# Dummy matmuls in TensorE's pauses, a reordered top-k schedule, and the first top-k quarter split by head, in a fused transformer and expert-lookup kernel

## The reference, cut to what matters

```python
def peer_ffn(h, wq, sub_keys, u, v):
    ...
        q = (xb @ wq).reshape(PEER_BLOCK, PEER_HEADS, 2, PEER_HALF)       # 128 tokens, 8 heads
        s = jnp.einsum('thpd,hpnd->thpn', q, sub_keys).astype(jnp.float32)
        s1, i1 = lax.top_k(s[:, :, 0], PEER_TOPK)                          # 16 of 128, twice
        s2, i2 = lax.top_k(s[:, :, 1], PEER_TOPK)
        cand = (s1[..., :, None] + s2[..., None, :]).reshape(PEER_BLOCK, PEER_HEADS, PEER_TOPK * PEER_TOPK)
        ...
        top, pos = lax.top_k(cand, PEER_TOPK)                              # 16 of 256
        eid = jnp.take_along_axis(cand_id, pos, axis=-1).reshape(PEER_BLOCK, PEER_HEADS * PEER_TOPK)
        g = jax.nn.softmax(top, axis=-1)...
        act = jax.nn.gelu(jnp.einsum('td,ted->te', xb, u[eid]))
        return jnp.einsum('te,ted->td', g * act, v[eid])
```

## Time and profile before

| what | value |
|---|---|
| median of 3 runs | 2390.88 us (2390.44 to 2392.16) |
| the profiled execution | 2392.13 us, of which the span is 2390.3 us |
| busy share: TensorE, VectorE, ScalarE, GpSimd | 85%, 63%, 32%, 42% |
| mean granted TensorE clock | 0.945 |
| DMA traffic | 777.33 MB, 325 GB/s over the span |
| gathers | 512, the first issued at 812.93 us, the last at 2361.44 us |
| first gather of chains 0, 1, 2, 3 | 812.93, 1171.60, 1601.95, 2041.33 us |

### The profile page before, as it was taken

How to read it: one execution, slowest core, us unless ns; L and a number is a source line. 1 busy time by engine, 2 the same in 40 slices (tenths; PEclk the granted TensorE clock), 3 DMA queues, 4 the chain that set the end, 5 groups by cost and what they waited for, 6 DMA issues and landing times.

```text
span 2390.3 us, 25020 instructions
## 1 busy us (share of the span) xinstructions
PE 2035.8 (85%) x8374; PEld 1293.0 (54%) x8374; DVE 1499.1 (63%) x3729; ACT 776.3 (32%) x1769; POOL 993.5 (42%) x693
## 2 busy tenths in 40 slices
PE   6999979998989899999778997877898878677876
PEld 3865759987867655543235645543564546232322
DVE  5654241215341577888677776769877868777755
ACT  2322234344312233333333242222333323233332
POOL 3720547788722133444333243333422333444542
PEclk8999999999999999999899998998998999999999
DMA  8445444445442699999999999999998999999997
GB/s 330 175 162 198 167 151 160 167 169 196 168 159 80 232 423 421 424 402 400 415 421 422 384 397 420 421 415 397 421 416 321 402 421 369 410 411 422 415 425 302
DMA packets 139760, 777.33 MB, mean 325 GB/s; under 512 B 15512, under 2 KB 17688, under 8 KB 73072
## 3 DMA queue, kind: packets, MB, share of 16 engines
q0 software_dynamic: 75792, 547.25, 55.7%
q1 hardware_dynamic: 63696, 228.44, 25.9%
q10 hardware_dynamic: 144, 0.05, 0.0%
HBM read 774.62 MB, written 1.06 MB: 325 GB/s over the span
## 4 chain that ended last, share of the span: by engine, by line
PE 47%; DVE 23%; DMA 22%; ACT 4%; issue 2%; POOL 2%; SPq 0%; DVEq 0%; ACTq 0%; POOLq 0%
PE banks L808 17%; PE banks L899 13%; DMA rows_c<-in_uv,p_eid 10%; DMA rows_b<-in_uv,p_eid 6%; PE banks L936 6%; DMA W<-in_weights 5%; DVE rows_b L2353 3%; PE banks L1111 2%; DVE rows_c L2353 2%; DVE arena L2353 2%; PE banks L973 2%; DVE arena L1928 2%; PE banks L1337 1%; DVE arena L1934 1%; ACT arena L1531 1%
## 5 line engine op out<-in xcount | busy, mean ns | idle before, releaser
L710 POOL TENSOR_TENSOR W_lo<-W,W_hi 128x1024 fp32r<-128x1024 f32 x160 | 391.9, 2456 | 190.1 <-ACT W_hi L1478 189.3
L899 PE MATMUL banks<-arena 128*128 128x512 f32 x696 | 346.1, 635 | 96.0 <-ACT arena L1540 95.7
L762 POOL DMA_INDIRECT arena<-in_uv,p_eid x192 | 221.1, 1151 | 484.7 <-PE banks L899 381.5
L899 PE MATMUL banks<-rows_b,arena 128*128 128x512 f32 x640 | 318.6, 638 | 61.8 <-ACT arena L1540 61.8
L762 POOL DMA_INDIRECT rows_b<-in_uv,p_eid x192 | 220.4, 1148 | 313.4 <-PE banks L899 223.5
L1529 ACT ACTIVATE arena<-arena 128x2 f32<-128x2 f32 x256 | 52.0, 203 | 854.6 <-DVE arena L1934 853.7
L2353 DVE SCALAR_TENSOR_TENSOR rows_b<-rows_b,H 128x1024 f32<-128x1024 f32 x192 | 232.6, 1224 | 115.5 <-DMA rows_b<-in_uv,p_eid 114.0
L2353 DVE SCALAR_TENSOR_TENSOR arena<-arena,H 128x1024 f32<-128x1024 f32 x192 | 232.6, 1224 | 82.3 <-DMA arena<-in_uv,p_eid 78.7
L899 PEld LDWEIGHTS banks<-arena 128*128 128x128 f32 x696 | 132.0, 200 | 268.7 <-issue 138.8
L1478 ACT ACTIVATE W_hi<-W 128x1024 fp32r<-128x1024 f32 x160 | 168.3, 1058 | 320.0 <-PE banks L808 218.9
L899 PE MATMUL banks<-rows_c,arena 128*128 128x512 f32 x440 | 218.1, 638 | 52.5 <-ACT arena L1540 52.4
(11 more groups left out here) (300 smaller groups left out, 3118.0 us busy)
## 6 DMA issues: line engine op xcount, KB each, us to landing
W<-in_weights SPq DMA_DIRECT2D x408, 512.0 KB, 4.7
gain<-in_rows SPq DMA_DIRECT2D x7, 512.0 KB, 13.3
gain<-in_rows POOLq DMA_DIRECT2D x6, 512.0 KB, 5.3
arena<-in_keys SPq DMA_DIRECT2D x3, 1024.0 KB, 10.0
arena<-in_uv,p_eid POOLq DMA_INDIRECT x192, 11.9
rows_b<-in_uv,p_eid POOLq DMA_INDIRECT x192, 12.4
arena<-in_rows POOLq DMA_DIRECT2D x1, 2048.0 KB, 13.4
rows_c<-in_uv,p_eid POOLq DMA_INDIRECT x128, 12.0
```

The source lines that it names most:

```text
L710: po.tensor_tensor(W_lo[:, slot, :], W[:, (PARTS * n + part) % RAW_RING, :], W_hi[:, slot, :].bitcast(F32), ALU.subtract).then_inc(S_("lo_ ...
L762: po.indirect_dma_start(rows[slot], None, io[f"uv{l}"], bass.IndirectOffsetOnAxis(ap=p_eid[:, t, j:j + 1], axis=0))\
L899: mm = pe.matmul(banks[:, plan.bank(f"p_v{c}", b), :], diag[:, m % DIAGS, :], rows[slot][:, D + b * BLK:D + (b + 1) * BLK], start=j == 0, ...
```

## The change

1. **Dummy matmuls.** A new function on TensorE, called ahead of thirteen waits of the program. Its matmuls multiply the identity by 512 constant columns in fp32, into the bank that the stage fills next, and their results are overwritten.
2. **T2.** The transposes of the normed memory tokens come after the eighth feed-forward tile instead of the fifth, on TensorE, VectorE and in the plan.
3. **Two gain loads.** GpSimd's `load_gain(5)` and `load_gain(6)`, which wait for norms, each come after one more tile's low halves.
4. **Hooks.** Chain 0's jobs move to earlier groups. In chain 2 the job (2, 3) has its lists at group 21 instead of 9, and the job (2, 2) its heads at group 10 instead of 26. The scores of the last quarter get a place of their own in the arena (16400), and ScalarE's `odd` waits for one list job fewer when `t` is 1.
5. **Rows on VectorE.** Chain 2 adds 18 rows on VectorE (groups 40 to 57) instead of 34 (3 to 12 and 34 to 57). The 16 others are weighed by TensorE.
6. **First quarter by head.** In chains 0, 2 and 3 the first job runs as lists, heads and keys of one head, then of the other, and `eid_ready` is signalled after each. GpSimd may issue 16 gathers after the first signal. `top16` waits for each instruction when it has one list alone.

```diff
+LISTS_AT = [{2: (0, 1), 13: (0, 2), 20: (0, 3), 26: (1, 0), 33: (1, 1), 40: (1, 2), 48: (1, 3)}, {},
+            {1: (2, 1), 6: (2, 2), 21: (2, 3)}, {1: (3, 1), 14: (3, 2), 28: (3, 3)}]
+HEADS_AT = [{g + 4: job for g, job in LISTS_AT[0].items()}, {}, {4: (2, 1), 10: (2, 2), 38: (2, 3)}, {4: (3, 1), 18: (3, 2), 32: (3, 3)}]
+ADDED_IN = [(), (*range(3, 13), *range(34, 58)), range(40, 58), ()]
...
-        if i == 4:
+        if i == 7:
             p.add("T2", 4)
...
-        p_qT, p_s = area(13840, 4, P), [area(9744 + 512 * n, 4, NK) for n in range(PH // 2)]
+        p_qT, p_s = area(13840, 4, P), [area(at, 4, NK) for at in (9744, 10256, 10768, 16400)]
...
+        def keys_at(c):
+
+            whole = list(range(0, SEL, 2 * PK))
+            return whole if c == 1 else [0, PK] + whole[1:]
...
             low("x_k0")
+            low("x_v0")
             load_gain(5)
-            low("x_v0")
+            low("e_pv")
             load_gain(6)
-            low("e_pv")
...
-                    if j % (2 * PK) == 0:
-                        po.wait_ge(S_("eid_ready"), c * (PH // 2) + j // (2 * PK) + 1)
+                    if j in keys_at(c):
+                        po.wait_ge(S_("eid_ready"), sum(len(keys_at(b)) for b in range(c)) + keys_at(c).index(j) + 1)
...
+            def busy(stage, n):
+
+                bank = claim(stage)
+                at, width = CONST["causal"]
+                for _ in range(n):
+                    pe.matmul(bank, ident, const[:, at:at + width], start=True, stop=True)
...
+                    if (name, u) == ("a", 0):
+                        busy("a_t0", 4)
...
+            busy("z_qk", 8)
+            busy("a_T", 2)
+            busy("m_cum", 2)
+            busy("mg_T", 1)
+            busy("w_out", 2)
+            busy("T1", 12)
             norm_T(1)
+            busy("ff_g0", 2)
+            busy("down", 4)
+            busy("x_k0", 6)
+            busy("e_pv", 2)
+                busy("T5", 6)
                 norm_T(5)
+                busy("x_q", 1)
...
-                act.wait_ge(S_("lists_ready"), (PH // 2) * c)
+                act.wait_ge(S_("lists_ready"), (PH // 2) * c - t)
...
+                issue = step.overlap if len(jobs) > 1 else step
...
+            def first_heads(c, work):
+
+                for h in range(2):
+                    top_lists(c, 0, h, h + 1)
+                    top_heads(c, 0, work, h, h + 1)
+                    top_keys(c, 0, work, h, h + 1)
```

More of the change, by code:

```diff
@@ L2594, in top16, with top_lists @@
                 for values, index, src, work in jobs:
-                    step.overlap(v.max(values[:, 8:16], work))
+                    issue(v.max(values[:, 8:16], work))
                 for values, index, src, work in jobs:
-                    step.overlap(v.max_index(index[:, 8:16], values[:, 8:16], work))
+                    issue(v.max_index(index[:, 8:16], values[:, 8:16], work))
                 step.all()
-            def top_lists(c, n):
+            def top_lists(c, n, first=0, end=2):
@@ L2602, in top_lists @@
                 after(v, f"p_s{n}.{c}")
                 b0, src, work = 4 * n, j_s[c][n] if c < 2 else p_s[n], p_work[c // 2]
-                top16([(p_v16[:, b0 + j, :], p_idx[:, j, :], src[:, j, :], work[:, j * NK:(j + 1) * NK]) for j in range(4)])
-                step(v.tensor_copy(p_i16[:, b0:b0 + 4, :], p_idx[:]), "lists_ready")
-            def top_heads(c, n, work):
-                h0 = 2 * n
-                v16 = p_v16.rearrange("p (h a) k -> p h a k", a=2)[:, h0:h0 + 2]
-                shape = [P, 2, PK, PK]
-                tt(p_cand[:].rearrange("p (h a b) -> p h a b", a=PK, b=PK), v16[:, :, 0, :].unsqueeze(3).to_broadcast(shape),
-                   v16[:, :, 1, :].unsqueeze(2).to_broadcast(shape), ALU.add)
-                cut = [slice(h * S, (h + 1) * S) for h in range(2)]
-                top16([(p_top[:, h0 + h, :], p_pos[:, h, :], p_cand[:, cut[h]], work[:, cut[h]]) for h in range(2)])
-                top = p_top[:, h0:h0 + 2, :]
-                tt(gates_of(c, n), top, top[:, :, 0:1].to_broadcast([P, 2, PK]), ALU.subtract, "top_ready")
+                lists = range(2 * first, 2 * end)
@@ new lines, in top_lists, with top_heads @@
+                top16([(p_v16[:, b0 + j, :], p_idx[:, j, :], src[:, j, :], work[:, j * NK:(j + 1) * NK]) for j in lists])
+                step(v.tensor_copy(p_i16[:, b0 + 2 * first:b0 + 2 * end, :], p_idx[:, 2 * first:2 * end, :]),
+                     "lists_ready" if end == 2 else None)
+            def top_heads(c, n, work, first=0, end=2):
+                h0, size = 2 * n + first, end - first
+                v16 = p_v16.rearrange("p (h a) k -> p h a k", a=2)[:, h0:h0 + size]
+                shape = [P, size, PK, PK]
+                tt(p_cand[:, 0:size * S].rearrange("p (h a b) -> p h a b", a=PK, b=PK), v16[:, :, 0, :].unsqueeze(3).to_broadcast(shape),
+                   v16[:, :, 1, :].unsqueeze(2).to_broadcast(shape), ALU.add)
+                cut = [slice(h * S, (h + 1) * S) for h in range(size)]
+                top16([(p_top[:, h0 + h, :], p_pos[:, h, :], p_cand[:, cut[h]], work[:, cut[h]]) for h in range(size)])
+                top = p_top[:, h0:h0 + size, :]
+                tt(gates_of(c, n)[:, first:end, :], top, top[:, :, 0:1].to_broadcast([P, size, PK]), ALU.subtract,
+                   "top_ready" if end == 2 else None)
@@ L2619, in gates_of, with top_keys @@
             def gates_of(c, n):
                 return p_g[:, CHAINS[c][1], 2 * PK * n:2 * PK * (n + 1)].rearrange("p (h k) -> p h k", h=2)
[L2623 to L2631 removed]
+            def top_keys(c, n, work, first=0, end=2):
+                t, n_top, size = CHAINS[c][1], (end - first) * PK, end - first
+                pos = p_pos[:, 0:size, :].rearrange("p h k -> p (h k)")
+                step.overlap(v.tensor_scalar(p_bits[:, 0, 0:n_top], pos, 4, None, ALU.logical_shift_right))
+                step(v.tensor_scalar(p_bits[:, 1, 0:n_top], pos, 15, None, ALU.bitwise_and))
+                step(v.tensor_copy(p_ab[:, :, 0:n_top], p_bits[:, :, 0:n_top]))
+                i16 = p_i16.rearrange("p (h a) k -> p h a k", a=2)[:, 2 * n + first:2 * n + end]
+                eq = [p_cand[:, 0:size * S], work[:, 0:size * S]]
@@ L2656, in queries @@
                 feed(4)
[L2657 to L2659 removed]
+                first_heads(c, p_work[1])
                 feed()
```

36 lines of the change are left out of this document (10 added, 26 removed).

## The result

The changed kernel takes 2376.65 us (median of four, 2374.9 to 2379.0), the one before 2391.5 beside it: ratio 0.9939, 95% interval 0.9924 to 0.9955, or 14.9 us less. I had forecast 2359, 31.5 us less. The direction and the range hold, the size is a little under half.

What follows compares the result with a forecast made beforehand. It took TensorE's sequence to bound the time before the first gather and DMA the time after. Terms 23 + 5.5 - 2 + 7.5 - 2.5 = 31.5 us off the median 2390.88 gave 2359 us, range 2343 to 2377.

Steps and rivals of the forecast that it cites:

- dummies, clock less overrun: First half, TensorE: 18 us saved by holding the clock (0 to 26), less 1 us for two overrun short pauses.
- T2: First half: transposes of the normed memory tokens three tiles later take 4.3 us of waits off TensorE's sequence.
- gain loads: First half: with the tile ahead of the load of gain 5, TensorE's 1.79 us wait goes, 1.8 us saved.
- first head earlier, chain 0: Chain 0's first job split by head: the first gather starts 5.5 us earlier (4.3 to 7.2), and that gain stays.
- split in chains 2 and 3: First jobs of chains 2 and 3: VectorE's block without dots grows 3.4 us; costs 2 us (0 to 6.8).
- new numbers in chain 2: Chain 2's hooks: heads at group 10 fill DMA's hole at 1800 to 1850, 7.5 us saved (0 to 9.5).
- 16 rows to TensorE: Chain 2: sixteen rows moved from VectorE add 27.5 us of TensorE work; costs 2.5 us (0 to 27.5).
- the cover is the wait itself: Cost of the dummies: twelve take 10.3 us in a pause of 11.2, six take 5.2 in 5.9.
- TensorE's dense query tiles space the rows there as well: Behind VectorE's longer block in chains 2 and 3: reason for taking 1.5 and 0.5 us, not 3.4 us.
- Most of a lag of a few us: Chain 2's moved rows: eight rows and six weight parts in flight (27 us) cover most of TensorE's late releases.
- A sign that I had named for an error: Prediction is wrong if first gather to end (1579 us) grows instead of shrinking by some 3 us.
- dummies that do not hold the clock: Rival, first half: the 18 us go and the 1 us cost stays, giving 2377 us; chance 0.09.

Runs made afterwards that it cites:

- d1: The kernel before with the 52 dummy matmuls alone (new function and its thirteen calls): 2381.9 us, ratio 0.9960.
- e5: The changed kernel without the eight dummies ahead of the first product (z_qk): 2370.9 us, ratio 0.9917.
- e7: The changed kernel without the dummies ahead of z_qk and with the split by head in chain 0 only: 2363.9 us, ratio 0.9879.
- e8: The changed kernel with T2 back behind the fifth feed-forward tile, dummies kept: 2376.7 us, one run.
- e12: The changed kernel with the split by head in chain 0 only and the gain loads in their old places: 2364.7 us, one run.
- d4: The kernel before with only the first top-k job of chains 0, 2 and 3 split by head: 2396.3 us, ratio 1.0024.
- e6: The changed kernel with the split by head in chain 0 only; chains 2 and 3 take both heads at once: 2368.4 us, ratio 0.9900.
- e13: The kernel before with the new group numbers, the fourth score area and ScalarE's wait, rows staying on VectorE: 2382.6 us, ratio 0.9963.
- e14: The kernel before with only the 16 rows of chain 2 moved to TensorE: 2398.9 us, ratio 1.0031.
- e16: The changed kernel, split kept, with ScalarE's first-job exponential behind the third query tile instead of the second and VectorE's gates one group later: 2376.1 us, ratio 0.9922.
- e9: The changed kernel, split in chain 0 only, dummies kept, GpSimd's first-product subtractions starting only after VectorE stored all four low halves: 2364.1 us, ratio 0.9884.
- e15_best: The changed kernel with split in chain 0 only, the 16 rows back on VectorE, and GpSimd's first subtractions behind VectorE's low halves: 2357.15 us, ratio 0.9861.
- e10_feed_between: Against e9: in chains 2 and 3's first job VectorE does one group of dots between lists and heads, one between heads and keys: 2365.3 us, ratio 0.9894.

## Why the prediction came out half

| term | forecast, us saved | measured | from |
|---|---|---|---|
| dummies, clock less overrun | 17 | 9.6 to 10.1; 13.7 without the call at z_qk | d1, with the 3.6 of e5 and e7 |
| T2 | 4.3 | 4.6 at the first MAX8 | e8 |
| gain loads | 1.8 | 0 | e12 |
| first head earlier, chain 0 | 5.5 | 5.5, of which some 1.4 are lost within chain 0 | d4's trace, lengths of chain 0 |
| split in chains 2 and 3 | -2 | -5 to -9 | e6 |
| new numbers in chain 2 | 7.5 | 8.8 | e13 |
| 16 rows to TensorE | -2.5 | -7.4 | e14 |

The measured ones sum to some 11 to 15 us, against 14.9 with an interval from 11 to 18.

**The clock: right, but one price was never put in.** The dummies hold the clock (1.00 from 347 to 417 us, where the earlier trace rows have 0.50 for 17 us), and the five low stretches left ahead of the first gather last 3.4 or 6.8 us each. With the call at z_qk out of the account, some 14 of the 17 us are there. Of the other 3 about one is counted with T2, whose 4.6 us are more than its 3.4 of waits; the rest is open. What failed is the step "the cover is the wait itself": I priced the dummies by the pause they fill and not by what starts earlier behind it. At z_qk the earlier product sends GpSimd's work back to back, and VectorE, which I had not looked at in this place, loses 4.4 us (13.43 against 9.04) and TensorE with it. I had this pair's contention in hand at T2, where I read 4.57 us for two instructions. The Trainium skill ("SBUF — State Buffer", SBUF: two separate sides) calls the port pair that VectorE and GpSimd share an exclusive lock, which a VectorE instruction with two SBUF inputs needs against a GpSimd instruction that reads SBUF. The blocking agrees with it (10.69 us where 0.69 is the price alone). By the Trainium skill the one that starts first gets the pair. That does not agree: by the records VectorE's instruction begins at 44.85 and GpSimd's subtraction at 45.59, and VectorE is the one that waits.

**The gain load: wrong.** The 1.79 us of TensorE's idling were read off the releaser of one row. GpSimd was the last to wait, but with the load out of its way it waits 6.05 us for ScalarE's high half, which ScalarE makes behind its own instructions of the same norm.

**The split in chains 2 and 3: mis-sized.** This step failed: "TensorE's dense query tiles space the rows there as well, so I take 1.5 us for chain 3 and 0.5 for chain 2". The whole cost is 5 to 9 us, about the 6.8 of two longer blocks of 3.4, which I had as the upper bound. The tiles do not cover it: as e16 and d4 show, the third of them is copied 2.3 us later, because ScalarE, which has to copy it, has the weights of the waiting dots in front of it in its program.

**The rows: mis-sized.** "Most of a lag of a few us" is covered where TensorE waits, and it was so for the ten rows I looked at. The step that failed is that I looked at those ten alone. The other six fall into a full product in front of a norm, where TensorE's time is the path.

**Right:** T2 (with part of the price in the clock), the first head in chain 0 (the split job takes 18.0 us where I had 17.8, and the first gather comes 9.2 us behind the first MAX8), and the numbers in chain 2, with their place. A sign that I had named for an error showed up as well: gather to end grew by 3.7 us in the trace, or by 1.3 in the means of the traces with the same code, instead of shrinking by 3. That the losses left the total inside the range is no merit of the sum: it stands 0.35 us under the upper end, which was set by a rival (dummies that do not hold the clock) that did not happen. The forecast's first gather was 784; it is 793.5, and 788.2 without the call at z_qk. The ninth gather comes 22 us behind the first and not 15: ScalarE takes four more banks of the query product, up to 810.2 us, before it makes the first weights, and the split doesn't move those. DMA does not run empty for it, its share is 1.02 from 803 to 838. Yet not all of "the 5.5 us stay". From its first gather to chain 1's, chain 0 takes 358.3 to 360.1 us in the twelve traces with its first job split and 357.0 to 358.7 in the six without, 1.4 us more in the mean.

## What to carry to other kernels

Price a filler by what it lets start earlier, not only by the pause that it fills: look at every engine that works in the few us behind it. A step that lengthens one engine's stretch can cost its full length where another engine has that stretch's results in its in-order program, and little where that engine waits anyway; so look at each place where the moved work lands, not at the fullest window alone. Try each part of a bundle by itself: here 9 us of a good part were hidden by 7 us of a bad one that had been added to help it.

## What the hardware showed that I had not expected

**VectorE blocked for the length of a run.** A 128x512 TENSOR_TENSOR of two SBUF inputs takes 0.69 us alone, 8.31 us beside three GpSimd subtractions in a row (e5) and 10.69 beside four. In these traces it doesn't slip in between two subtractions that follow each other within 0.1 us, and is through where GpSimd idles for 0.25 us.

**The clock behind a short pause.** In e9 TensorE idles 2.95 us at 48.51, in the changed kernel 2.16 us at 48.09, after the same eight dummies. Window of e9_pool_waits, then of the changed kernel:

```profile
48.00:54.50 6.50, 5.99 (x28) 6.02 (x29) 0.00 (x0) 0.50 (x1) 5.03 (x3) 0.50 1.00 419
```

```profile
48.00:54.50 6.50, 5.98 (x48) 5.81 (x48) 6.50 (x1) 1.46 (x2) 6.50 (x3) 1.00 0.98 416
```

Under 1 us more of idling goes with 1.2 GHz instead of 2.4 for 6.8 us, 28 matmuls where 48 were done. The two other kernels with this code show it too: e15_best idles 3.06 us and has 6.8 us at 1.2 GHz, e10_feed_between 2.53 us and 3.4. No run shows whether a ninth dummy would have kept the clock.
